# Value projections of two mixers with the tokens as stationary operand and the weights streaming

## The reference, cut to what matters

```python
h = rmsnorm(x, norm_mix_g[layer])
p = h @ w_in                     # even: q, k, v, ig, fg, og, z, xbc, dt; odd: q, k, v, g
# even: v has A_HEADS * A_DV = 4 * 256 columns; odd: v has C_HEADS * C_DV = 8 * 256 columns
s   = einsum('blhd,bshd->bhls', qc, kc) * w_in
num = einsum('bhls,bshv->bhlv', s, vc) + ...        # values used token by token
C_new = C * decay + einsum('bshd,bshv->bhdv', kc * g, vc)
```

## Time and profile before

| | |
|---|---|
| time, median of 3 runs | 1037.89 us (1037.03 to 1038.46) |
| the profiled execution's own time | 1032.65 us |
| its span | 1030.9 us |
| mean granted TensorE clock | 0.984 |
| PE busy | 991.7 us, 96% |
| DVE busy | 747.9 us, 73% |
| ACT busy | 559.2 us, 54% |
| POOL busy | 381.0 us, 37% |
| HBM traffic | 171 GB/s over the span |

### The profile page before, as it was taken

One profiled execution on the slowest core, in us unless ns is written; L12 is line 12 of the kernel. 1 busy time (PEld: TensorE's weight loads), 2 busy tenths in 40 slices (PEclk: granted clock), 3 DMA queues, 4 the chain that ended last, 5 costly groups with the idle time before them and its releaser, 6 DMA issues.

```text
span 1030.9 us, 19172 instructions
## 1 busy us (share of the span) xinstructions
PE 991.7 (96%) x7256; PEld 939.5 (91%) x7256; DVE 747.9 (73%) x1326; ACT 559.2 (54%) x932; POOL 381.0 (37%) x599
## 2 busy tenths in 40 slices
PE   7989999898899999999999999999999999999996
PEld 6989888777589999999999999899989999999996
DVE  5776788877866999996458857677765699999442
ACT  6536666633544766555444356666645566665431
POOL 4003223224211777772005521322222377777100
PEclk9999999999899999999999999999999999999998
DMA  8463464453555554545444735776635455544541
GB/s 295 140 242 123 129 210 131 153 187 108 168 180 185 173 175 165 164 164 180 163 164 164 266 126 189 219 236 183 206 133 187 161 172 170 169 166 165 179 144 46
DMA packets 64684, 177.22 MB, mean 172 GB/s; under 512 B 5888, under 2 KB 24064, under 8 KB 64592
## 3 DMA queue, kind: packets, MB, share of 16 engines
q1 hardware_dynamic: 64304, 174.86, 51.0%
q0 software_dynamic: 288, 1.12, 0.3%
HBM read 154.92 MB, written 21.05 MB: 171 GB/s over the span
## 4 chain that ended last, share of the span: by engine, by line
PE 85%; DVE 6%; ACT 4%; issue 3%; POOL 1%; DMA 1%; SPq 0%; DVEq 0%; ACTq 0%; POOLq 0%
PE bank L809 25%; PE bank L811 24%; PE bank L810 24%; PE bank L855 2%; ACT wh L1227 2%; DVE wl L1633 1%; PE bank L1165 1%; PE bank L1133 1%; DMA raw<-wts 1%; PE bank L1095 1%; PE bank L867 1%; POOL sts L2353 1%; PE bank L876 1%; PE bank L875 0%; PE bank L1139 0%
## 5 line engine op out<-in xcount | busy, mean ns | idle before, releaser
L1227 ACT ACTIVATE wh<-raw 128x1024 fp32r<-128x1024 f32 x257 | 270.5, 1057 | 318.3 <-PE bank L811 317.6
L1633 DVE TENSOR_TENSOR wl<-raw,wh 128x1024 fp32r<-128x1024 f32 x257 | 321.3, 1254 | 164.4 <-ACT wh L1227 162.4
L809 PE MATMUL bank<-hH,wh 128*128 128x288 f32 x1160 | 352.9, 304 | 7.1 <-DVE wl L1633 4.8
L810 PE MATMUL bank<-hL,wh 128*128 128x288 f32 x1160 | 345.5, 298 | 0.0
L811 PE MATMUL bank<-hH,wl 128*128 128x288 f32 x1160 | 344.3, 297 | 0.0
L809 PEld LDWEIGHTS bank<-hH,wh 128*128 128x128 f32 x1160 | 221.0, 191 | 10.7 <-DVE wl L1633 3.4
L810 PEld LDWEIGHTS bank<-hL,wh 128*128 128x128 f32 x1160 | 221.2, 191 | 0.6
L811 PEld LDWEIGHTS bank<-hH,wl 128*128 128x128 f32 x1160 | 221.5, 191 | 0.0
L1756 DVE SCALAR_TENSOR_TENSOR cy<-pad,vec,cy 128x304 f32<-128x304 f32 (+1 forms) x212 | 139.5, 659 | 4.5 <-ACT cy L1275 0.6
L2194 POOL COPY pad<-fst 128x16 f32<-128x16 f32 x88 | 94.3, 1076 | 67.7 <-DVE cy L1756 67.7
L809 PE MATMUL bank<-upH,wh 128*128 128x288 f32 x352 | 104.4, 297 | 0.0
(11 more groups left out here) (336 smaller groups left out, 1605.7 us busy)
## 6 DMA issues: line engine op xcount, KB each, us to landing
raw<-wts SPq DMA_DIRECT2D x257, 512.0 KB, 3.3
st<-r_in SPq DMA_DIRECT2D x9, 512.0 KB, 6.5
r_out<-st SPq DMA_DIRECT2D x9, 512.0 KB, 4.4
st<-c_in SPq DMA_DIRECT2D x8, 514.0 KB, 6.8
c_out<-st SPq DMA_DIRECT2D x8, 514.0 KB, 5.0
sts<-h_in SPq DMA_DIRECT2D x12, 256.0 KB, 5.1
h_out<-sts SPq DMA_DIRECT2D x12, 256.0 KB, 2.6
st3r<-r_in SPq DMA_DIRECT2D x4, 512.0 KB, 6.0
```

The lines of the kernel that those rows point to most:

```text
L809: mm(out, h, xh, start=(k == 0), stop=False)
L810: mm(out, h, xl, start=False, stop=False)
L1227: s.do(act(wh[:, c % RING, :], raw[:, c % RING, :], ACT.Copy), hi_ready)
L1633: do(tt(wl[:, c % RING, :], raw[:, c % RING, :], wh[:, c % RING, :].bitcast(F32), ALU.subtract), lo_ready)
```

## The change: what it does

Two neighbouring value tiles (256 weight columns, one head) are computed together and token-major. For each k the stationary operand is a block of 128 tokens of hH or hL, and 256 weight columns move: for each of the two token blocks high x high, low x high and high x low, so six matmuls, into the two halves of one bank. The 32 sample tokens use a second bank: a new array xs holds high and low sample tokens side by side (64 stationary columns), against wh and against wl, two matmuls; rows 0 to 31 of the result are the high tokens' product and rows 32 to 63 the low tokens'. A pair is 8 x 8 = 64 matmuls of 256 columns in place of 2 x 24 of 288. Weights on the host are laid so that one chunk holds four k of both tiles, and the two chunks are worked off where the two tiles were. Both banks are claimed at the start of the pair's first half.

rstd is needed per token as a column now: it is turned once per mixer (job rc0 after even tile 5, rc2 after odd tile 4) and three small DVE copies put it in rcol. DVE empties a pair in one go after its second half, in `values`, straight into vA or rvA. The transposes, vT, rvT and the copies of turned blocks are gone. ACT fills xs by two ACTIVATEs per mixer.

```diff
+RCOL = {"even": START["even"] + 5, "odd": START["odd"] + 4}
@@ PE
+            def value_half(n, t, xs):
+                half, c = TILES[t][2] % 2, place(t, 0)[0]
+                if half == 0:
+                    claim(t)
+                    claim(t + 1)
+                    pe.wait_ge(xs_ready, n + 2)
+                out, smps, x = mb(t - half), mb(t - half + 1), operand_of(n)
+                pe.wait_ge(lo_ready, c + 1)
+                for i in range(4):
+                    k = 4 * half + i
+                    (xh, xl), w = x(k), slice(2 * i * P, 2 * (i + 1) * P)
+                    h, lo = wh[:, c % RING, w], wl[:, c % RING, w]
+                    for g in range(2):
+                        tok, to = slice(g * P, (g + 1) * P), out[:, g * AV:(g + 1) * AV]
+                        mm(to, xh[:, tok], h, start=(k == 0 and g == 0), stop=False)
+                        mm(to, xl[:, tok], h, start=False, stop=False)
+                        mm(to, xh[:, tok], lo, start=False, stop=(k == KD - 1 and g == 1))
+                    mm(smps[0:2 * NS, 0:AV], xs[:, k, :], h, start=(k == 0), stop=False)
+                    last = mm(smps[0:2 * NS, 0:AV], xs[:, k, :], lo, start=False, stop=(k == KD - 1))
+                last.then_inc(gemm_done, 1)
...
-                wait_empty(pe, f"v{2 * h + 1}")
+                wait_tile_empty(pe, VALUE[2 * h + 1])
...
-                tiles([t], operand_of(0))
+                if t in VALUE:
+                    value_half(0, t, xsA)
+                else:
+                    tiles([t], operand_of(0))
-                if t - 1 in VALUE:
-                    n = VALUE.index(t - 1)
-                    wait_tile_empty(pe, t - 1)
-                    turn(f"v{n}", vT[:, n % 2, :])
+                if t == RCOL["even"]:
+                    pe.wait_ge(rstd_ready, 1)
+                    turn("rc0", rstd)
...
-            def turn_value(n):
-
-                wait_tile_empty(pe, RV[n])
-                turn(f"rv{n}", rvT[:, n % 2, :])
...
             for t in range(O + 2, O + LEAD):
-                tiles([t], operand_of(2))
+                if t in RV:
+                    value_half(2, t, xsR)
+                else:
+                    tiles([t], operand_of(2))
+                if t == RCOL["odd"]:
+                    pe.wait_ge(rstd_ready, 3)
+                    turn("rc2", rstd)
                 if t == O + LEAD - 2:
                     front("r", 0, qk_r)
-                    turn_value(0)
-            turn_value(1)
             for h in range(CH):
                 group(h, 0)
                 intra(h)
                 if h:
                     updates(h - 1, LATE_STATES)
                 group(h, 1)
-                if h + 1 < CH:
-                    turn_value(2 * h + 2)
                 chunk_products(h)
                 group(h, 2)
                 if h + 1 < CH:
-                    turn_value(2 * h + 3)
                     front("r", h + 1, qk_r)
@@ ACT
+            def side_by_side(n, xs):
+
+                eng.wait_ge(xlo_ready, KD * (n + 1))
+                for i in range(2):
+                    s.do(act(xs[:, :, i * NS:(i + 1) * NS], H[n][i][:, :, TP:T].bitcast(F32), ACT.Copy), xs_ready)
@@ DVE
+            def row_columns(name):
+
+                wait_job(eng, name)
+                b = mb(name)
+                do(copy(rcol[:, 0:2], b[:, 0:TP].rearrange("p (g n) -> p g n", g=2)[:, :, 0]))
+                do(copy(rcol[NS:2 * NS, 2:3], b[0:NS, TP:TP + 1]))
+                do(copy(rcol[0:NS, 2:3], b[0:NS, TP:TP + 1]), mix_dve)
+                settle()
+
+            def values(t, dst):
+
+                wait_tile(eng, t)
+                for g in range(2):
+                    do(ts(dst(g), mb(t - 1)[:, g * AV:(g + 1) * AV], rcol[:, g:g + 1], None, ALU.mult), gemm_dve if g else None)
+                b = mb(t)
+                do(ts(dst(2)[0:NS], b[NS:2 * NS, 0:AV], rcol[NS:2 * NS, 2:3], None, ALU.mult))
+                settle()
+                do(stt(out=dst(2)[0:NS], in0=b[0:NS, 0:AV], scalar=rcol[0:NS, 2:3], in1=dst(2)[0:NS],
+                       op0=ALU.mult, op1=ALU.add), gemm_dve)
...
                 elif kind == "v":
-                    scaled(t, vT[:, i % 2, :])
+                    if i % 2:
+                        values(t, lambda g: values_a(i // 2, g)[:, 0:AV])
...
                 elif kind == "rv":
-                    scaled(t, rvT[:, i % 2, :])
+                    if i % 2:
+                        values(t, lambda g: rvA[:, i // 2, g, :])
@@ host
-    def ordered(w, tiles):
-
-        return weight_tiles(w).reshape(len(tiles), KD, P, P)[tiles].reshape(-1, P, P)
+    def ordered(w, tiles, values):
+
+        out = weight_tiles(w).reshape(len(tiles), KD, P, P)[tiles]
+        for n in values:
+            out[n:n + 2] = out[n:n + 2].swapaxes(0, 1).reshape(2, KD, P, P).copy()
+        return out.reshape(-1, P, P)
```

More of the change, by code:

```diff
@@ L264, in plan_banks @@
         tile(group_tile(h, 0))
+        if turns_left:
+            tile(group_tile(h, 1))
         job(f"roi{h}", "act", "five")
@@ L268, in plan_banks @@
             late_states(job, h - 1, "five")
-        tile(group_tile(h, 1))
-        if turns_left:
-            job(f"rv{2 * h + 2}", "dve", "five")
+        if not turns_left:
+            tile(group_tile(h, 1))
         job(f"ro1{h}", "act", "five")
@@ L297 @@
 GATES = START["even"] + EVEN.index(("gates", 0))
+RV = [START["odd"] + ODD.index(("rv", i)) for i in range(2 * CH)]
+RCOL = {"even": START["even"] + 5, "odd": START["odd"] + 4}
 def group_tile(h, step):
@@ L392, in build @@
         rstd = keep.take("rstd", [P, T])
+        rcol = keep.take("rcol", [P, 4])
         conv = Area(keep.at)
@@ L488, in build @@
         st_r = st + [odd.take(f"st{i}r", [P, 4, AV + 1]) for i in (3, 4)]
-        rvT = odd.take("rvT", [P, 2, T])
+        xsR = odd.take("xsR", [P, KD, 2 * NS], F32R)
         gT = nc.alloc_sbuf_tensor_at("gT", [P, 8, T], F32, offset=keep.at)
@@ L637, in build @@
         OG = [T0 + EVEN.index(("og", i)) for i in range(8)]
-        RV = [START["odd"] + ODD.index(("rv", i)) for i in range(16)]
         HEADS = [("a", h, h) for h in range(AH)] + [("r", h, AH + h) for h in range(CH)]
@@ L1428, in _ @@
                     gate_exponentials()
+                if t == T0 + 2:
+                    side_by_side(0, xsA)
                 if t > T0:
@@ L1920, in _ @@
                     gate_columns()
-                if t - 2 in VALUE:
-                    value_a(VALUE.index(t - 2))
+                if t == RCOL["even"] + 1:
+                    row_columns("rc0")
             for h in range(AH):
@@ L2119, in _ @@
                 split(last_chunk(t) + 3)
+                if t == RCOL["odd"] + 1:
+                    row_columns("rc2")
             front("r", 0, AH)
-            value(0)
             for h in range(CH):
@@ L2124, in _ @@
                 step(h, 0)
-                if h == 0:
-                    value(1)
-                else:
+                if h:
                     sample_out(h - 1)
@@ L2477 @@
     w_even = np.concatenate([w[:, :2048], gates, w[:, 2056:5640]], axis=1)
-    streams = [ordered(w_even, even_tiles), halves(a["even_w_out"][0]),
+    streams = [ordered(w_even, even_tiles, [t - START["even"] for t in VALUE[::2]]), halves(a["even_w_out"][0]),
                weight_tiles(paired(a["ffn_w_up"][0])), weight_tiles(a["ffn_w_down"][0]),
-               ordered(a["odd_w_in"][0], odd_tiles), halves(a["odd_w_out"][0]),
+               ordered(a["odd_w_in"][0], odd_tiles, [t - START["odd"] for t in RV[::2]]), halves(a["odd_w_out"][0]),
                weight_tiles(paired(a["ffn_w_up"][1])), weight_tiles(a["ffn_w_down"][1])]
```

25 lines of the change are left out of this document (9 added, 16 removed).

## The result

The changed kernel takes 1046.36 us, the median of 6 runs (1044.21 to 1049.19). The kernel before took 1037.46 us in the same comparison (6 runs, 1033.93 to 1038.46). The ratio is 1.0091 [1.0070, 1.0112]: 9.4 us slower by the ratio (8.9 between the medians), with an interval of 7 to 12 us. The forecast was 1045.6, 7.7 us slower. So the size came out, but not all of its terms did; the rest of this text is about which.

A forecast was written before the change was run, and what follows sets the result against it. PE, busy 96% of the span, was taken as the bound. Streams 14.2, removed turns -7.9, rstd turns 0.7, moved wait 0.0 and clock 0.7 gave +7.7 us on 1037.89: 1045.6 us, range 1039.5 to 1053.5.

The forecast's parts named there:

- The streams: PE, twelve value pairs: 64 matmuls of 256 columns at 118.5 ns replace 48 of 288; +14.2 us.
- Rival 1: Sample products on PE: 64-column stationary operands drain the array, 0.2 us per shape change, +38 us, about 1083; 11%.
- Rival 2: All 768 new matmuls: 256 columns stream at one per cycle, 106.7 ns each, about 1035.8 us; 8%.
- The turns: PE, value tiles of both mixers: 24 turns removed at 0.33 us each, -7.9 us; two of rstd added, +0.7.
- The odd mixer: Odd value tiles, PE busy without a gap: eight pairs' streams less 16 turns plus one of rstd, +4.5 us.
- The wait that moves: Even mixer: PE's standing moves from the first turn to v0, waiting for k2's bank; 0.0 us by itself.
- whatever PE does: Even mixer: DVE reaches k2 at 47.00 regardless of PE; row_columns adds 0.4 us, so v0 starts about 47.9.
- Rival 3: Even pairs and end of gates: PE waits on DVE for the two banks, plus a second clock drop, about 1053; 6%.
- The clock term: Even mixer: the longer single gap at v0 may lower PE's granted clock; half a drop, +0.7 us (0 to 1.5).
- FFN stretches as before: Both FFNs: a sign of being right was that their stretches stay unchanged; no term in the sum.

The follow-up runs named there:

- e9: Changed kernel without the sample tokens' products against the low weights, 96 matmuls fewer; 1036.49 us in one execution, beside 1032.73 for the kernel before.
- e11: Kernel before with each value turn's three transposes issued twice; 1038.38 us in one execution, beside 1035.00.
- e2: The change in the odd mixer alone, even mixer as in the kernel before; 1041.44 us, ratio 1.0069.
- e3: Changed kernel with the second bank claimed only after the products of the first four k, ahead of the sample products; 1041.76 us, ratio 1.0057 to the kernel before.
- e1: The change in the even mixer alone, odd mixer as in the kernel before; 1040.30 us, ratio 1.0045.
- e5: Kernel before plus an unused array of 32 bytes per partition where the change puts rcol; 1039.61 us against 1036.82, ratio 1.0030.
- e6: Changed kernel with rcol at the top of SBUF, so arrays behind rstd keep their old addresses; 1042.32 us, ratio 1.0062 to the kernel before.
- e10: Kernel before, meant to issue value turns twice, but the edit never took hold, so the kernel before again; 1034.38 us, beside 1032.73.
- e8: Kernel before plus an unused array of 64 bytes per partition where the change puts rcol; 1038.62 us in a single execution.

## Why the prediction was right, step by step

**The streams** held. PE's timeline in an odd value half shows starts 0.11 to 0.12 us apart, narrow stationary operand or not:

```profile
600.59 0.28 PE L837 MATMUL bank<-wl,hH 128*128 128x256 f32 x1
600.71 0.28 PE L838 MATMUL bank<-wh,xsR 128*64 128x256 f32 x1
600.83 0.28 PE L839 MATMUL bank<-wl,xsR 128*64 128x256 f32 x1
600.94 0.28 PE L835 MATMUL bank<-wh,hH 128*128 128x256 f32 x1
```

A half takes 3.79 to 3.80 us, so a pair 7.59 (forecast 7.58). This ends two rivals. Rival 1 wanted some 0.3 us at every change to 64 columns; the row shows 0.12 before and 0.12 to 0.11 after, and e9 0.117 for each. The Trainium skill, "TensorEngine Tiling (Array Packing)", section "Key Properties", says that a change of tiling mode drains the engine. No drain shows here: a float32r product with 64 stationary columns between full ones doesn't behave as such a change. The same page of the Trainium skill, section "Gotcha 2: Feature Incompatibilities", names float32r only for transposes, so it doesn't settle why. Rival 2, one column per cycle, wanted 0.107.

**The turns** held: 0.33 forecast, 0.335 in e11. So did their like for rstd: the odd mixer's first stretch, tile 4 to the first state product of head 0, grew from 53.24 to 54.69 us, +1.45, and the sum of one and a half pairs (+1.77), two turns (-0.66) and the added turn (+0.33) is 1.44.

**The odd mixer** follows from both. The two products between which e11 was measured, of the kernel before and then of the changed kernel (PE's timeline, first state product of head 0 and of head 7):

```profile
604.60 0.64 PE L1133 MATMUL bank<-st3r,qTm 128*32 128x256 f32 x8
...
747.69 0.64 PE L1133 MATMUL bank<-st,qTm 128*32 128x256 f32 x8
```

```profile
613.12 0.64 PE L1155 MATMUL bank<-st3r,qTm 128*32 128x256 f32 x8
...
759.37 0.64 PE L1155 MATMUL bank<-st,qTm 128*32 128x256 f32 x8
```

143.09 us became 146.25, +3.16. Six and a half pairs less 14 turns by the forecast's prices give 3.1. Over the whole odd mixer it is 4.67 (forecast 4.5). e2 and e3 have 146.25 and 146.45 between the same two products; e1 and e5, with the odd mixer as before, have 143.09.

**The wait that moves** was right in place, cause and nearly in size. PE's timeline around v0, with the first matmul of v2, and then DVE's:

```profile
44.37 0.29 PE L814 MATMUL bank<-hH,wl 128*128 128x288 f32 x1
48.42 0.55 PE L835 MATMUL bank<-wh,hH 128*128 128x256 f32 x1 [3.75 <-DVE kT L1696]
...
61.83 0.28 PE L835 MATMUL bank<-wh,hH 128*128 128x256 f32 x1
```

```profile
43.71 0.16 DVE L1711 COPY rcol<-bank 128x2 f32<-128x2 f32 x1
...
47.88 0.44 DVE L1696 TENSOR_TENSOR kT<-bank,rstd 128x288 f32<-128x288 f32 x1
```

v0 starts at 48.42 (forecast 47.9) after 3.75 us for k2's bank. DVE empties that bank from 47.88 where it was 47.00. The copies into `rcol` took 0.55 us of that, to 44.26 (forecast 0.4). The other 0.33 us had come before them: DVE's scan ahead of the copies starts at 42.93 for 42.60. So "whatever PE does" was not quite true of DVE's 47.00. That this is the turn of rstd on PE, of the same length, is likely but was not followed. Rival 3, waits at the later even pairs, didn't come: the only other wait of PE on value work in the even mixer is one of 0.2 us.

**The clock term was mis-sized for the trace, and its cover for the timed runs.** I put 0.7 us on half a drop. The drop came whole. From 48.40 to 54.10 there are 26 matmul starts, where 5.70 us at 0.1185 would hold 48; 22 starts less are 2.6 us. v2 then starts at 61.83 for a forecast of 58.8: 0.5 by the wait, 2.6 by the clock. In the timed runs the even mixer cost much less than the +5.6 of the trace: +2.2 in e1 (4.7 less 2.5), and +1.7 in e6 (6.4 less 4.7), with some 2 us of uncertainty in each; at equal clock 2.0 and 1.9. The forecast was 3.2, of which 2.4 were streams and turns. The reason is that the kernel before loses clock too, here or elsewhere, as in e10 and e8. Beside e1 its mean clock was 0.9814 over 19 executions, and e1's was 0.9811 over 7: by 0.8 us for each 0.001 that is 0.2 us. So the trace, where one execution of each is compared, shows a clock term of 2.6 us, and the timed runs of e1 show next to none. The profiled execution of the kernel before, at 0.984 and 5.2 us below the first median, was one of the faster ones.

**"FFN stretches as before" failed.** This is the step that was wrong: +2.5 us, from 32 bytes of layout, in no term of the sum. e5 shows it without the change (+3.1 timed), e6 shows the change without it. So the total of +9.4 is 4.7 for the odd mixer, 2.5 for the addresses and about 2.2 for the even mixer, where the forecast had 4.5, nothing, and 3.2. It was right in direction and cause. But the total came nearer than its terms did: the even mixer was put 1.0 us too high, half of that by the clock term, and the addresses were left out. That these two have opposite signs was luck.

## What to carry to other kernels

Before turning a product round, count streamed columns on the engine that is bound. A few extra tokens that ride at the end of a 288-column stream cost 48 x 32 columns per pair of tiles; as a stationary operand of their own they need 16 x 256, and that was more than the saved transposes. Where a wait stands on a full engine, look first for what can be claimed or turned later: moving one turn by one tile gave 3.6 us (2.3 at equal clock) without any change of layout, and beat both kernels. List the mean granted clock beside each time: here it moves one kernel's time by more than several of the edits did, and a single profiled execution can be 5 us away from the median. Put a new small array behind everything else, or time the kernel before with an unused array of its size, before you put a difference down to the change.

## What the runs showed of the hardware that was not expected

- The spacing of float32r matmuls depends on where their operands lie in SBUF: 3.173, 3.200 or 3.227 us for the same tile of 24 matmuls with a shift of 64, 0 or 32 bytes, 2.5 us over this kernel for 32 bytes and nothing in sum for 64. The rule behind it stays open.
- A float32r product with 64 stationary columns between full ones streams 256 columns in the same 0.117 to 0.12 us as they do.
- The granted clock of one stretch differs between executions of one program. The kernel before had 1.00 in the stretch behind its first turn in one execution and 0.50 for 3.4 us in the other. Over 43 executions its mean clock went from 0.977 to 0.986, and its time fell by some 0.8 us for each 0.001. The clock's chance, not only its size, belongs in such a forecast.
